# A decoder step on one core: the samples' query from narrow products, and key units that follow it

## Time and profile before

| what | us |
|---|---|
| median of the runs | 667.61 |
| the profiled execution | 666.25 |
| its span, first to last instruction | 664.4 |
| busy in the span: TensorE | 562.7 |
| VectorE | 371.5 |
| ScalarE | 136.2 |
| GpSimd | 129.8 |

### The profile page before, as it was taken

One profiled execution on the slowest core, in us unless ns is written; L12 is line 12 of the kernel. 1 busy time (PEld: TensorE's weight loads), 2 busy tenths in 40 slices (PEclk: granted clock), 3 DMA queues, 4 the chain that ended last, 5 costly groups with the idle time before them and its releaser, 6 DMA issues.

```text
span 664.4 us, 7517 instructions
## 1 busy us (share of the span) xinstructions
PE 562.7 (85%) x2900; PEld 317.7 (48%) x2900; DVE 371.5 (56%) x679; ACT 136.2 (20%) x267; POOL 129.8 (20%) x116
## 2 busy tenths in 40 slices
PE   3998889989999467988979997797998989788882
PEld 1775567877888424446468445332322323222220
DVE  4069999999999998820423144734342442414124
ACT  3013401115211144451610021110101111010102
POOL 1625441111111877772000000000000000000001
PEclk9999989999999567985999999798999999999997
DMA  8999768798874948999469983469999999999951
GB/s 311 398 357 334 288 235 325 291 402 299 289 281 133 378 153 314 422 423 394 172 163 408 384 340 106 148 220 417 419 420 418 421 420 421 420 420 421 407 233 68
DMA packets 66318, 213.83 MB, mean 322 GB/s; under 512 B 15379, under 2 KB 17955, under 8 KB 58092
## 3 DMA queue, kind: packets, MB, share of 16 engines
q1 hardware_dynamic: 52108, 137.46, 53.2%
q0 software_dynamic: 11392, 73.41, 28.8%
q10 hardware_dynamic: 2784, 2.51, 1.1%
HBM read 208.76 MB, written 4.60 MB: 321 GB/s over the span
## 4 chain that ended last, share of the span: by engine, by line
PE 44%; DVE 24%; SPq 10%; DMA 7%; ACT 6%; issue 5%; POOL 3%; ACTq 1%; DVEq 0%
PE PS L619 7%; SPq L469 7%; DVE arena L1734 6%; PE PS L1185 6%; DVE x_rows L1738 6%; PE PS L1167 5%; PE PS L1080 4%; PE PS L1095 4%; PE PS L1193 3%; DMA arena<-in_w_down 3%; SPq L474 3%; PE PS L1233 3%; DMA arena<-in_w_up 2%; POOL arena L549 2%; POOL temp L549 1%
## 5 line engine op out<-in xcount | busy, mean ns | idle before, releaser
L619 PE MATMUL PS<-xT,arena 128*128 128x264 f32 x608 | 145.6, 399 | 0.8 <-ACT arena L1376 0.5
L619 PEld LDWEIGHTS PS<-xT,arena 128*128 128x128 f32 x608 | 116.8, 195 | 26.4 <-issue 4.7
L1734 DVE TENSOR_TENSOR arena<-arena,x_rows 128x2048 f32<-128x2048 f32 x32 | 73.1, 2283 | 21.2 <-ACT x_rows L1328 21.1
L1738 DVE TENSOR_REDUCE x_rows<-arena 128x32 f32<-128x2048 f32 x32 | 73.2, 2287 | 1.1
L549 POOL DMA_INDIRECT arena<-in_cache_k_b,unit_idx x32 | 44.6, 1395 | 138.9 <-DVE x_rows L1738 134.5
L1193 PE MATMUL PS<-temp 128*128 128x512 f32 (+1 forms) x96 | 48.9, 646 | 12.4 <-DVE temp L2261 8.1
L1185 PE MATMUL PS<-arena,temp 128*32 128x512 f32 x384 | 48.0, 644 | 9.3 <-DMA arena<-in_w_up 4.8
L609 POOL TENSOR_TENSOR small<-small,consts 128x1 f32<-128x1 f32 x3 | 2.6, 868 | 241.2 <-DVE small L2297 241.2
L2237 DVE TENSOR_TENSOR x_rows<-PS,x_rows 128x512 f32<-128x512 f32 (+1 forms) x48 | 32.9, 687 | 24.4 <-PE PS L1193 24.3
L549 POOL DMA_INDIRECT arena<-in_cache_v_b,unit_idx x32 | 34.9, 1090 | 29.6 <-PE PS L1025 13.4
L2261 DVE COPY temp<-PS 128x512 f32<-128x512 f32 x8 | 5.5, 691 | 55.1 <-PE PS L1233 55.1
(11 more groups left out here) (374 smaller groups left out, 804.2 us busy)
## 6 DMA issues: line engine op xcount, KB each, us to landing
arena<-in_w_down SPq DMA_DIRECT2D x32, 1024.0 KB, 15.9
arena<-in_w_gate SPq DMA_DIRECT2D x48, 512.0 KB, 13.1
arena<-in_w_up SPq DMA_DIRECT2D x48, 512.0 KB, 13.6
arena<-in_w_in SPq DMA_DIRECT2D x9, 2048.0 KB, 11.3
temp<-in_w_gate SPq DMA_DIRECT2D x12, 512.0 KB, 14.8
temp<-in_w_up SPq DMA_DIRECT2D x12, 512.0 KB, 14.7
temp<-in_w_out SPq DMA_DIRECT2D x1, 4096.0 KB, 15.3
x_rows<-in_x_prompt SPq DMA_DIRECT2D x2, 1024.0 KB
```

The lines of the kernel that those rows point to most:

```text
L619: last = nc.tensor.matmul(PS[0:m, n % 2, 0:T], w[:, k, c0:c0 + m], xT[:, k, :], start=(k == 0), stop=(k == KC - 1))
L1734: nc.vector.tensor_tensor(k_ring[:, u], k_ring[:, u], q_all[:, b % 2:b % 2 + 1, :].to_broadcast([P, 4, H * HD]), ALU.mult).then_inc(s_mul, 1)
L1738: nc.vector.tensor_reduce(z_s[:, b, :].rearrange("p (h r) -> p r h", r=R)[:, 4 * u:4 * u + 4, :], k_ring[:, u].rearrange("p r (h d) -> p r ...
```

## The change

- A new product for the samples alone: `xs_pad` holds the 8 columns of the samples, padded with zeros to 32, and eight products of 128x32 by 128x512 with `w_a` (four row groups of PSUM, `start=(k < 4)`) give four partial sums of the query, `four_q`. Its scaled copy is spread and summed in one step by `pick_q`, made of the constant `fold`. So x of the samples is loaded, squared, scaled and turned first, and the 8 sample columns no longer wait for chunks 0 to 3.
- The order of the chunks is now q_i (0 to 3), k_i and w_i (4), q_b (5 to 8), and then as before.
- The constants are loaded in two pieces; the first has 292 columns. `w_ki` is loaded by ScalarE's queue.
- VectorE: `bias_blocks` (the zeroed table, its four copies and four memsets) moves from the start to behind unit 3. 4 units, then 4, then 6 stand before the search (14 in all, 11 before), one in each of 16 rounds, and one each ahead of `search_taken` and `list_places`; none after.
- Value units v0 to v3 go to `k_ring` and wait only for key units 28 to 31; v4 to v7 go to `v_ring`, behind the wait for N_ALL and the memset. `w_pa` and `w_pb` change halves, and expert 2 is loaded first.
- Gate chunks 13, 14 and 15 move behind `list_before`, `after_keys` and `list_buckets`, on TensorE and on ScalarE.
- WEXP and NEWREL move to another PSUM bank, and the wait for `s_wcol` moves with them.

```diff
         @block.sync
         def _(sp):
+            sp.dma_start(x_rows[0:NS, 2, :], a["x_sample"].rearrange("b o d -> (b o) d")).then_inc(s_xs, 16)
+            sp.dma_start(page_of[:, :], a["pages"]).then_inc(s_page, 16)
+            sp.dma_start(consts[:, 0:FIRST], a["shape_consts"][:, 0:FIRST]).then_inc(s_const, 16)
             sp.dma_start(x_rows[:, 0:2, :], a["x_prompt"][0].rearrange("(t p) d -> p t d", p=P)).then_inc(s_x, 16)
-            sp.dma_start(consts[:, :], a["shape_consts"]).then_inc(s_const, 16)
-            sp.dma_start(w_a[:, :, :], w_in[:, :, O_QB:O_QB + 512]).then_inc(s_wa, 16)
+            sp.dma_start(w_a[:, :, :], w_in[:, :, O_QB:O_QB + 512]).then_inc(s_wa, 16)
...
             sp.dma_start(w_b[:, :, :], w_in[:, :, O_QI:O_QI + 512]).then_inc(s_wb, 16)
-            sp.dma_start(w_ki[:, :, 0:HD], w_in[:, :, O_KI:O_QB]).then_inc(s_wki, 16)
+            sp.dma_start(consts[:, FIRST:], a["shape_consts"][:, FIRST:]).then_inc(s_const2, 16)
...
+            sp.wait_ge(s_proj, N_QA)
+            sp.dma_start(w_a[:, :, :], w_in[:, :, O_QA:O_QA + 512]).then_inc(s_wa, 16)
...
             def fetch_v(n):
                 if n >= 8:
                     pool.wait_ge(s_vused, n - 7)
-                elif n >= 4:
-                    pool.wait_ge(s_kused, 4 * NS - 7 + n)
+                elif n < 4:
+                    pool.wait_ge(s_kused, 4 * NS - 3 + n)
...
-            pool.wait_ge(s_proj, N_ALL)
             for n in range(4):
                 fetch_v(n)
+            pool.wait_ge(s_proj, N_ALL)
             nc.gpsimd.memset(a_pads[0], 0.0).then_inc(s_apad0, 1)
             fetch_v(4)
             fetch_v(5)
...
+            turn_x(0)
+            turn_x(1)
+            pe.wait_ge(s_xT, 1)
             pe.wait_ge(s_wa, 16)
+            for k in range(KC):
+                rows = slice(k % 4 * 32, k % 4 * 32 + 32)
+                last = nc.tensor.matmul(PS[rows, 2 + M_Q % 2, :], xs_pad[:, k, :], w_a[:, k, :],
+                                        start=(k < 4), stop=(k >= 4))
             last.then_inc(s_tr, 1)
             pe.wait_ge(s_pick, 1)
             spread_q(0)
...
+            list_before()
             gate(13)
-            gate(14)
-            list_before()
-            gate(15)
             list_told()
             prompt_a_scores(0)
             after_keys(0)
+            gate(14)
             new_key()
             list_buckets()
+            gate(15)
...
+            pe.wait_ge(s_evac, N_ALL)
             values(0, 3)
...
+            act.dma_start(w_ki[:, :, 0:HD], w_in[:, :, O_KI:O_QB]).then_inc(s_wki, 16)
+            act.dma_start(w_ki[:, :, HD:HD + H], w_in[:, :, O_WI:O_KI]).then_inc(s_wki, 16)
...
             for k in range(4):
                 unit(k)
+            bias_blocks()
...
-            for k in range(4, 7):
+            for k in range(4, 8):
                 unit(k)
...
-            for k in range(7, 11):
+            for k in range(8, 14):
                 unit(k)
             search_form()
             search_ask(0)
             for i in range(ROUNDS):
-                unit(11 + i)
+                unit(14 + i)
...
-            unit(11 + ROUNDS)
+            unit(14 + ROUNDS)
             search_taken()
-            unit(12 + ROUNDS)
+            unit(15 + ROUNDS)
             list_places()
-            unit(13 + ROUNDS)
             softplus_keys(0)
             list_rows()
-            unit(14 + ROUNDS)
-            unit(15 + ROUNDS)
             later_keys(0)
```

More of the change, by code:

```diff
@@ L75, in shape_constants @@
         "ident": np.eye(P),
+        "fold": (i[:, None] % 32 == np.arange(32)[None, :]).astype(float),
+        "half": np.full((P, 3), -0.5),
+        "row_block": (i % RB).astype(float)[:, None],
         "negones": -np.ones((P, P)),
@@ L625, in count_above, with spread_q, turn_x @@
                 nc.tensor.matmul(COUNT, const("ones"), count_s, start=True, stop=True).then_inc(s_ctot, 1)
-            pe.wait_ge(s_const, 16)
[L628 to L641, removed]
+            def spread_q(b):
+                m = M_QB[b]
+                pe.wait_ge(s_trf, max(m - 1, M_Q + 1))
+                nc.tensor.matmul(PS[:, 2 + m % 2, :], pick_q[:, b, :], four_q, start=True, stop=True).then_inc(s_tr, 1)
+            def turn_x(t):
+                pe.wait_ge(s_xn, t + 2)
+                for half in range(2):
+                    for c in range(4):
+                        d0 = (half * 4 + c) * P
+                        last = nc.tensor.transpose(PS[:, ACC + 2 * t + half, c * P:(c + 1) * P],
+                                                   xn_rows[:, t, d0:d0 + P], ident)
+                    last.then_inc(s_xtr, 1)
+            pe.wait_ge(s_const, 16)
+            pe.wait_ge(s_xn, 1)
             for c in range(KC):
@@ L690, in score_kidx @@
                 last.then_inc(s_kT_used, 1)
+            for c in range(4):
+                project_qb(c)
+            pe.wait_ge(s_const2, 16)
             pe.wait_ge(s_evac, N_KI + 1)
@@ L1328, in spread_q @@
                 nc.scalar.copy(q_all[:, b % 2, :], PS[:, 2 + m % 2, :]).then_inc(s_trf, 1)
+            act.wait_ge(s_tr, M_Q + 1)
+            nc.scalar.activation(four_q, PS[:, 2 + M_Q % 2, :], ACT.Copy, scale=HD ** -0.5).then_inc(s_trf, 1)
+            act.wait_ge(s_xn, 3)
             spread_q(0)
-            for c in range(4):
+            act.wait_ge(s_brow, 1)
+            nc.scalar.copy(bias_row, PS[:, 0, :]).then_inc(s_browc, 1)
+            for c in range(3):
                 evac(N_QI + c, qiT[:, c, :])
             spread_q(1)
+            evac(N_QI + 3, qiT[:, 3, :])
             act.wait_ge(s_proj, N_KI + 1)
@@ L1337, in _ @@
             nc.scalar.copy(wiT, PS[HD:HD + H, N_KI % 2, 0:T]).then_inc(s_evac, 1)
+            for c in range(4):
+                evac(N_QB + c, qbT[:, c, :])
             act.wait_ge(s_tr, M_WI + 1)
@@ L1454, in _ @@
             spread_q(7)
-            for c in range(10, 15):
+            for c in range(10, 13):
                 gate(c)
             list_told(M_BEFORE, from_before)
-            gate(15)
+            gate(13)
             list_told(M_TOLD, find[:, 1344:1632])
@@ L1718, in _ @@
+            dve.wait_ge(s_rstd, 2)
+            for t in range(2):
+                nc.vector.tensor_scalar(xn_rows[:, t, :], x_rows[:, t, :], rstd[:, t:t + 1], None, ALU.mult
+                                        ).then_inc(s_xn, 1)
+            dve.wait_ge(s_tab33, 16)
+            nc.vector.tensor_copy(table_wide[:, :].rearrange("p (h c) -> p h c", h=H),
+                                  table33[:, :].unsqueeze(2).to_broadcast([NB + 1, H, P // H])).then_inc(s_ones33, 1)
             for g in range(4):
@@ L1724, in _, with bias_blocks @@
                                         ALU.mult).then_inc(s_xT, 1)
-            dve.wait_ge(s_xtr, 5)
-            nc.vector.tensor_tensor(xT[:, :, NP_TOK:T], PS[:, 2, 0:KC * NS].rearrange("p (c n) -> p c n", c=KC),
-                                    g1T[:, :].unsqueeze(2).to_broadcast([P, KC, NS]), ALU.mult).then_inc(s_xT, 1)
+            dve.wait_ge(s_tr, M_Q + 1)
+            nc.vector.memset(xs_pad[:, :, 0:NS], 0.0)
+            def bias_blocks():
+                link(nc.vector.memset(bias_b4[:, :, :], 0.0))
+                diagonal = lambda rows, k: bias_b4[rows, :, :].rearrange("p q (e x) -> p (q e) x", e=2)[
+                    :, 0:4:3, k * H:(k + 1) * H]
+                for k in range(4):
+                    link(nc.vector.tensor_copy(diagonal(slice(k * NB, (k + 1) * NB), k),
+                                               table33[0:NB, :].unsqueeze(1).to_broadcast([NB, 2, H])))
+                for k in range(4):
+                    last = nc.vector.memset(diagonal(slice(k * NB, k * NB + 1), k), NEG)
+                last.then_inc(s_table, 1)
```

115 lines of the change are left out of this document (49 added, 66 removed).

## The result

The kernel after took 692.91 us (median of 4 runs, 690.87 to 696.06) beside 667.56 for the kernel before (4 runs, 665.04 to 670.08): ratio 1.0384, 95% interval 1.0328 to 1.044. It is 25.4 us slower. The forecast was 675.1 with a range to 684: the direction held, the size did not.

The account below looks back on a forecast made before the run. VectorE's and GpSimd's chains run side by side from 214 to 294 us, the later one counting; GpSimd's was forecast to slip 8.9 + 1.0 + 1.7 - 4.1 = 7.5 us, giving 675.1 us on the median, range 664 to 684.

Parts of the forecast that it names:

- The start: First key units on VectorE: query ready at 20 to 23 us, units bounded by key gathers, starting 12.6 us earlier.
- TensorE does not spoil this: Before the search: TensorE's stream lasts as long, loses some work, and still waited 2.58 us for the first count.
- the term for the later search: VectorE before the search: units start 12.6 us earlier but three more (13.6 us) stand ahead; search 1.0 us later.
- the gain of the list: VectorE's list: units taken out shorten it by 13.6 us, so its successors could be 11 to 12 us earlier.
- The queue: GpSimd's queue: gates 14 and 15 end 14.6 us after list_places, so memset and chosen-key gathers start 8.9 us later.
- the clock: TensorE at gates 14 and 15: a lowered granted clock adds 1.7 us, bounds 0 and 7.
- Back-pressure: GpSimd's gathers: only two megabytes of values in front instead of six, saving 4.1 us, bounds 0 and 6.
- One for one to the end: From the last gather of chosen values: TensorE's value work, projections and experts shift by the same time.
- The late start (1): At the start: small packets on ScalarE's queue delay w_a and every gather by 5.2 us; 680.3 us, chance 0.18.
- Rival 2: Whole kernel unchanged: start 4 us early, full clock, 5 us of back-pressure gone; 667.6 us, chance 0.18.
- Rival 3: VectorE's chain, not GpSimd's, sets the end, so its 11 us gain arrives; 656.6 us, chance 0.12.
- rival 4: At the start: gathers, not the query, set the first units; in full, units 3 us later, 678 us, chance 0.04.

Follow-up runs that it names:

- e1: The changed kernel with spread queries 2, 3, 6 and 7 placed earlier on TensorE and ScalarE; 677.75 us, ratio 1.0145 to the kernel before.
- e3: The kernel before with gates 13 to 15 moved late and the wait for all evictions before the first values; 680.26 us, ratio 1.0186.
- e2: As e1, with gates 13 to 15 back where the kernel before has them; 666.82 us, ratio 0.9994 to the kernel before.

## Why the prediction was right or wrong

- **The start** held. First unit 24.09 (said: 24, and 23 to 26), set by the landing of the keys; unit 4 at 46.05 (46). The narrow product took 2.94 us instead of 1.8, hidden as the text had it.
- **"So the search starts 1.0 us later than now ... TensorE does not spoil this"** is the step that failed: the term for the later search was set at 1.0 us, and waits of VectorE on TensorE's order were set at nothing. The first count came 10.4 us later: 9.3 of it is the wait for spread 2, and the rest, 1.1, is this term. I had looked at TensorE's length and at its wait for the first count, and not at where in its order the operands of the moved units are made. Two more such waits, 6.9 and 2.9 us, followed during the search, where the text had none. Together 19.1 us. With the spreads in time (e1) the first count is at 94.82, where the text had 95. By the same waits the gain of the list stayed out: VectorE's prompt scores began at 242.68, where the text had 10 us before 234.85; in e1 they began at 224.98.
- **The queue.** Gate 15 ended 13.6 us behind `list_places`; the text had 14.6 and 1.7 for the clock. In the changed kernel gate 13 ran while VectorE was still at `list_places`, and took 6.37 us at a granted clock of 0.59; gates 14 and 15 ran at 3.81 and 3.73, with a clock of 1.00. So the lower clock, which the text had laid on gates 14 and 15 from the slices of the kernel before, fell on a gate outside this path and cost nothing there. In e1 gate 14 took 5.94 us and gate 15 3.73, 2.2 together above the full clock (1.7 in the text), and the end was 16.8 us behind. The memset was 7.7 us later against `list_places` (said: 8.9 + 1.7).
- **Back-pressure:** from memset to last gather 69.84 us instead of 73.73, 3.9 less (4.1). The size held, the reason is not shown. In e3 six megabytes of values stand in front of the gathers of keys as in the kernel before, and none of the first eight of these took more than 1.24 us; from memset to last gather it is 69.50 us there. In e2 only two stand there, and one fetch of values of 2.95 us comes ahead of the memset, with 5.9 us of idle time before it. What makes a single issue long stays open; that the term came out right is in part luck.
- **One for one to the end:** held, 24.3 at the last gather, 24.6 at the projections, 25.4 in the medians.
- The sum with what was measured: 1.1 + 19.1 + 7.7 - 3.9 = 24.0; the text had 1.0 + 8.9 + 1.7 - 4.1 = 7.5. The whole difference is the 19.1, less 2.9 that the queue cost less.
- **Rivals.** The late start (1) did not come: w_ki's two issues took 0.60 us each on ScalarE's queue, and w_a landed 0.8 us earlier than before (GpSimd's first gather, which waits for it, is at 15.20, 16.00 in the earlier trace rows; the text had 2 to 3 us). Rival 2 needed the start 4 us early; it was not, and the memset was 28 us late. Rival 3 fell by its own sign: it wanted the memset out by 220, and it came at 248.40; VectorE's 11 us never arrived either. Of rival 4 the mild form came, as forecast: the first unit waited for its gather. The range left out the true time because no rival stood for a new wait of the moved units on their own operands.

## What to carry to other kernels

When units of work are moved forward on one engine, write down for each what it reads and where that is made in the written order of every other engine; the move is worth only what the last of these allows. A producer may be moved too early as well: it then blocks its engine until the buffer that it overwrites is free. And in a queue that issues gathers for many stages, a wait placed ahead of work that is ready delays all of it; here putting a wait, a memset and two fetches behind sixteen gathers gave back 7 us (2 to 13).

## What the runs showed of the hardware

The landing of w_ki in the kernel after (from the view of transfers, 1 to 22 us: last number, us from issue to landing):

```profile
w_ki<-in_w_in ACTq DMA_DIRECT2D x1, 256.0 KB, 4.1
```

In the kernel before it was 21.5 us, issued at 5.99 behind megabytes on the same queue. In the kernel after the same 256 KB went out on a queue of their own and landed in 4.1 us, with x (issued at 2.10) and the first weights (2.58) under way on SP's queue. The Trainium skill, page "DMA: Bandwidth & Descriptors", section "Queues, rings and completion order", says that the transfer engines take turns between queues; both landings fit that. They do not prove it, because w_ki was also issued ahead of these two (1.24), and no run separates its queue from its place in time.

The narrow products took 184 ns each at the start (2.94 us for 16) and 114 ns later in the kernel before (3.64 for 32), both at a granted clock of 1.00; why is open.

A chunk, 16 products in the trace, took what the granted clock of its stretch allowed:

| kernel | chunk | stretch | granted clock | us |
|---|---|---|---|---|
| after | gate 13 | 228.5 to 234.9 | 0.59 | 6.37 |
| after | gates 14 and 15 | 239.8 to 248.4 | 1.00 | 3.81, 3.73 |
| e1 | gate 13 | 210.8 to 216.2 | 0.71 | 5.34 |
| e1 | gate 14 | 223.2 to 229.2 | 0.63 | 5.94 |
| e1 | gate 15 | 230.2 to 233.9 | 1.00 | 3.73 |

For the three slow ones 3.75 us divided by the granted clock gives 6.4, 5.3 and 6.0. Both gates 13 come right behind idle time of TensorE (2.58 and 5.25 us) and two short products. Gate 14 of e1 stands behind the products with 18 columns and slower ones, without idle time of more than a microsecond; gate 14 of the kernel after stands behind the same products, with gate 13 and no idle time before them, and ran at 1.00. In the kernel before TensorE worked without idle time from 80 to 86 us at 1.00, on products with 8 columns at the end, and the chunk behind them (5.51 us) had 0.68. What moved the clock in these cases is not shown.
